# Attention with the values stationary and the turned exponentials moving, in a four-block kernel on one core

## The chip, the core and the metric

The kernel runs on one core of one Trainium2 chip. The core has TensorE (PE in the profile; its weight loads are listed as PEld and overlap it), VectorE (DVE), ScalarE (ACT), GpSimd (POOL) and SyncE (SP), each with its own instruction stream; they meet at semaphores. Matmuls write to PSUM, which has eight banks of 128 partitions by 512 words. The metric is the device time of one execution in microseconds (us).

## The reference, cut to what matters

The program computes a short gated convolution block with its MLP, an even block (attention beside a pooling path), a feed-forward block, a conformer block and another feed-forward block, on 512 positions of 1024 channels, all in float32. The change is inside the even block's attention, which has 8 heads of 64 channels and a decay that depends on the position:

```python
def forgetting_attention(q, k, v, f_logit, q_g, k_g):
    q = rms_norm(q, q_g); k = rms_norm(k, k_g)
    c = jnp.cumsum(jax.nn.log_sigmoid(f_logit), axis=1)
    ...
        s = einsum("bhqd,bhkd->bhqk", q_blk, k_h) * scale
        s = s + cq_blk[..., :, None] - c_k[:, :, None, :]
        s = where(k_pos <= q_pos, s, -inf)
        p = softmax(s, axis=-1)
        return einsum("bhqk,bhkd->bhqd", p, v_h)

def even_mixer(h, ...):
    ...
    return concatenate([a_out, p_out], axis=-1) @ w_out
```

## The kernel before, in words

Channels lie on partitions and positions on the free axis, except in attention, where a block of 128 queries lies on partitions. Weights come in units of 1024 x 256 in float32. ACT rounds each unit to a high half (`hi_half`, two copies of 128x1024 a unit), DVE computes the low half (`lo_half`), and PE forms three products for each (high x high, high x low, low x high). Attention itself runs in plain float32, for which PE issues two weight loads and two matmuls where the program has one.

All engines follow orders written out by hand. The attention stage is a loop of steps `s`, four to a head: step `s = 4h + q` is query block `q` of head `h`, and the causal mask leaves `(q + 1) * 128` keys to it. I call the steps q0 to q3, and the last block's turned exponentials "block q3". The stages are pipelined by hand over the steps:

- PE (lines 1837 to 1879): at step s the scores of s (stationary QS, moving KS, L1851) and the mask (L1852) into one of three banks; the turning of the exponentials of step s-2, block by block of 128 keys, by transposes into bank 4 or 5 (L1860); the product with V of step s-3 (L1871), in which the turned exponentials are stationary and V's 64 columns move, `q + 1` matmuls for a step, into bank 6 or 7. At four steps a pool product (L1879) follows.
- DVE (L1360 to L1383): the row minimum of step s (L1362; the scores are negated), a reciprocal of the sum (L1365), and the scaled output copied to `OT` (L1370). For heads 2 to 7 it also scales the queries and keys (`scaled_head`, L1306 and L1308), two full operations a head.
- ACT (L750 to L785): the copy of the turned exponentials from PSUM to `PT` (L756), the exponential with the row sum as a by-product (L771, an ACTIVATE and a read of the accumulator), for heads 2 to 7 the decay rows of queries and keys (`decay_rows`, L747 and L748: one partition of 512), and copies for the pooling path (L781).

After the loop PE runs the first four chunks of one output unit (24 matmuls, L1896 to L1898), turns `OT` by 16 transposes (L1907) so that channels lie on partitions again, and goes on with the output projection; ACT and DVE split the turned result into halves `HH` and `HL` (L785, L1383).

Which order the engines keep is the text of these loops; a wait names the count of another engine's semaphore. ACT and DVE work through their own lists in order, so an instruction that waits holds up all behind it.

Of the kernel before, what the change touches and what calls it, by code (L numbers as in the profile page):

```python
# [27 lines left out]
P = 128  # L28
T = 512
# [89 lines left out]

SUMMED_BY_PE = (ST_X0, ST_X1, ST_X2)  # L120
# [18 lines left out]
S_BANKS, POOL_BANK = (0, 1, 2), 3  # L139


def program(nc, i, out):
    ctx = ExitStack()
    with ctx:
# [12 lines left out]
        OT = at("OT", 16, [P, TB, T])  # L157
# [22 lines left out]
        V = at("V", 164.5, [P, TB, T])  # L180
# [11 lines left out]
        QS = at("QS", 172.5, [97, 2, T])  # L192
        KS = at("KS", 176.5, [97, 2, T])
        PR = at("PR", 180.5, [P, 2, T])
        PT = at("PT", 188.5, [P, 2, T])
# [59 lines left out]
        a_qk, a_row = sem("head_qk"), sem("head_decay_rows")  # L255
        a_s, a_min, a_e, a_rr = (sem("attn_" + x) for x in ("scores", "min", "exp", "recip"))
        a_t, a_tc, a_o, a_oe = (sem("attn_" + x) for x in ("turned", "copied", "out", "out_copied"))
        a_ot, a_h = sem("attn_out_turned"), sem("attn_out_hi")
# [31 lines left out]
        def first_unit(u, i):  # L290

            k = slice(2 * i, 2 * i + 2)
            if u < 2:
                return RAW[:, 1 - u, k, :], WH[:, 1 - u, k, :], WL[:, 1 - u, k, :]
            return RAW_3[:, k, :], WH_3[:, k, :], WL_3[:, k, :]

# [4 lines left out]
        def _(sp):  # L301
# [119 lines left out]

# [36 lines left out]
        def _(pool):  # L458
# [54 lines left out]

            pool.wait_ge(a_s, 8 * (HEADS // 2))
# [40 lines left out]
        def _(act):  # L555
# [194 lines left out]
            def turned_exponentials(k):  # L750

                n = (k % 4 + 1) * P
                act.wait_ge(a_t, k + 1)
                if k >= 2:
                    act.wait_ge(a_o, k - 1)
                act.activation(PT[:, k % 2, 0:n], PS_[:, 4 + k % 2, 0:n], ACT.Copy).then_inc(a_tc, 1)  # L756

            decay_rows(0)
            decay_rows(1)
            act.wait_ge(s_rc, 1)  # L760
            act.wait_ge(s_mm, U_EVEN + 8)
            for b in (2, 3):
                act.activation(V[:, b, UW:2 * UW], PS_[:, 3, b % 2 * UW:b % 2 * UW + UW], ACT.Copy, scale=sc_(S_RT + b)
                               ).then_inc(s_vr, 1)
            for s in range(4 * HEADS + 2):
                if s >= 2:
                    turned_exponentials(s - 2)
                if s < 4 * HEADS:
                    n = (s % 4 + 1) * P
                    act.wait_ge(a_min, s + 1)  # L770
                    act.activation(PR[:, s % 2, 0:n], PS_[:, S_BANKS[s % 3], 0:n], ACT.Exp, scale=-1.0,  # L771
                                   bias=sc_(S_MN + s % 8), accum_out=sc_(S_RS + s % 8)).then_inc(a_e, 1)
                if s == 3 or s == 6:
                    hi_half(U_EOUT + 1, 1, s // 6)
                if s % 4 == 1 and 5 <= s < 4 * HEADS - 4:
                    decay_rows(s // 4 + 1)
                if s % 4 == 3 and 11 <= s < 27:
# [172 lines left out]
        def _(dve):  # L950
# [43 lines left out]
            def split(m, gs=None, gain=None, k=0):  # L994
# [8 lines left out]
                for c in range(DC):  # L1003
# [307 lines left out]
            for p in range(8):  # L1311
# [16 lines left out]
                else:  # L1328
                    dve.wait_ge(s_rc, 1)
                    for b in range(TB if p == 6 else 2):  # L1330
                        ins = dve.tensor_scalar(V[:, b, (p - 6) * UW:(p - 5) * UW],
                                                PS_[:, 2 * j + b // 2, b % 2 * UW:b % 2 * UW + UW], sc_(S_RT + b), None,
                                                ALU.mult)
# [24 lines left out]
            for s in range(4 * HEADS + 4):  # L1358
# [4 lines left out]
                if 2 <= s < 4 * HEADS + 2:  # L1363
                    dve.wait_ge(a_e, s - 1)
                    dve.reciprocal(sc_(S_RR + (s - 2) % 8), sc_(S_RS + (s - 2) % 8)).then_inc(a_rr, 1)  # L1365
                if s >= 4:
                    k = s - 4
                    dve.wait_ge(a_o, k + 1)
                    dve.wait_ge(a_rr, k + 1)
                    dve.tensor_scalar(OT[:, k % 4, k // 4 * DH:k // 4 * DH + DH], PS_[:, 6 + k % 2, 0:DH],  # L1370
                                      sc_(S_RR + k % 8), None, ALU.mult).then_inc(a_oe, 1)
# [9 lines left out]
            for c in range(4):  # L1381
                dve.wait_ge(a_h, c + 1)
                tt(HL[:, c, :], PS_[:, 4 + c, :], HH[:, c, :].bitcast(F32), ALU.subtract).then_inc(s_x, 1)  # L1383
# [714 lines left out]
```

## Time and profile before

| | |
|---|---|
| Median of 3 runs | 1735.19 us (1731.91, 1735.19, 1735.36) |
| The profiled execution | 1731.89 us, span 1730.1 us |
| PE busy | 1709.8 us, 99% of the span |
| DVE, ACT, POOL busy | 1090.4, 693.2, 153.9 us |
| Attention, first score load to last product with V | 701.7 to 756.3 us of the span |
| DMA | 176.22 MB, mean 102 GB/s |

"Busy" for PE includes a modelled tail of each matmul, so that a busy PE can still have waited. The distance between the starts of two instructions tells more: a block that issues every 0.22 us although each matmul is listed with 0.39 us is a pipelined one. The granted clock of PE is given in parts of its full speed.

### The profile page before, as it was taken

What the parts mean: (1) busy time and instruction counts of PE and PEld (TensorE: products, weight loads), DVE (VectorE), ACT (ScalarE), POOL (GpSimd) and SP (SyncE); (2) the same over time, 40 slices, a digit from 0 to 9 for tenths busy, and PEclk for the clock granted to TensorE, in tenths of its full rate; (3) what the DMA queues carried; (4) which work ended last, traced back from release to release, by engine and by line L of the source; (5) the groups of instructions that cost most, each with busy time, mean ns of one, the idle gap of its engine ahead of it and who ended that gap; (6) DMA issues with size and microseconds to landing.
All of it is one profiled execution on the core that took longest, in us unless ns stands there. A gap on an engine that the chain in (4) does not pass through costs nothing.

```text
span 1730.1 us, 21548 instructions
## 1 busy us (share of the span) xinstructions
PE 1709.8 (99%) x7716; PEld 1382.4 (80%) x7716; DVE 1090.4 (63%) x1657; ACT 693.2 (40%) x1006; POOL 153.9 (9%) x142
## 2 busy tenths in 40 slices
PE   8999999999999999999999999999999999999999
PEld 7888878888888778888888888877656888888888
DVE  6799885353535573746663663669998666366364
ACT  4322353232323334744432432447666443243242
POOL 0000300000000040000000000005892000000000
PEclk9999999999999999999999999999999999999999
DMA  8566414323333132103232232232210323223222
GB/s 292 180 222 221 140 50 146 98 97 97 116 97 98 49 90 82 49 1 100 97 111 82 97 102 93 85 109 73 74 49 25 111 96 110 76 96 113 80 85 86
DMA packets 182338, 176.22 MB, mean 102 GB/s; under 512 B 3304, under 2 KB 181740, under 8 KB 182268
## 3 DMA queue, kind: packets, MB, share of 16 engines
q1 hardware_dynamic: 182268, 175.29, 31.7%
q8 instruction: 43, 0.70, 0.2%
q14 instruction: 27, 0.22, 0.0%
HBM read 173.15 MB, written 2.10 MB: 101 GB/s over the span
## 4 chain that ended last, share of the span: by engine, by line
PE 88%; DVE 9%; issue 1%; ACT 1%; DMA 1%; SPq 0%; DVEq 0%; ACTq 0%
PE PSUM L1546 23%; PE PSUM L1547 23%; PE PSUM L1548 23%; DVE PSUM L1478 4%; DVE WL L957 1%; PE PSUM L1871 1%; PE PSUM L1851 1%; PE PSUM L1896 1%; PE PSUM L1898 1%; PE PSUM L1897 1%; PE PSUM L1578 1%; PE PSUM L1632 1%; PE PSUM L1579 1%; PE PSUM L1580 1%; PE PSUM L1663 1%
## 5 line engine op out<-in xcount | busy, mean ns | idle before, releaser
L564 ACT ACTIVATE WH<-RAW 128x1024 fp32r<-128x1024 f32 x274 | 281.5, 1052 | 733.8 <-PE PSUM L1548 690.7
L1546 PE MATMUL PSUM<-XH,WH 128*128 128x512 f32 x1152 | 450.3, 391 | 0.0
L1548 PE MATMUL PSUM<-XH,WL 128*128 128x512 f32 x1152 | 448.2, 389 | 0.0
L1547 PE MATMUL PSUM<-XL,WH 128*128 128x512 f32 x1152 | 448.2, 389 | 0.0
L957 DVE TENSOR_TENSOR WL<-RAW,WH 128x1024 fp32r<-128x1024 f32 x274 | 341.3, 1268 | 10.5 <-ACT WH L564 10.5
L1546 PEld LDWEIGHTS PSUM<-XH,WH 128*128 128x128 f32 x1152 | 216.2, 188 | 46.2 <-issue 1.2
L1547 PEld LDWEIGHTS PSUM<-XL,WH 128*128 128x128 f32 x1152 | 216.2, 188 | 45.7 <-issue 1.2
L1548 PEld LDWEIGHTS PSUM<-XH,WL 128*128 128x128 f32 x1152 | 216.2, 188 | 45.1
L1546 PE MATMUL PSUM<-HH,WH 128*128 128x512 f32 x644 | 251.3, 390 | 0.4
L1548 PE MATMUL PSUM<-HH,WL 128*128 128x512 f32 x644 | 250.6, 389 | 0.0
L1547 PE MATMUL PSUM<-HL,WH 128*128 128x512 f32 x644 | 250.6, 389 | 0.0
L1401 DVE TENSOR_TENSOR ZP<-PSUM,R 128x512 f32<-128x512 f32 x88 | 56.7, 687 | 176.7 <-PE PSUM L1548 176.7
L1546 PEld LDWEIGHTS PSUM<-HH,WH 128*128 128x128 f32 x644 | 120.9, 188 | 27.5 <-DVE HL L1425 2.1
L1548 PEld LDWEIGHTS PSUM<-HH,WL 128*128 128x128 f32 x644 | 120.9, 188 | 25.2
L1547 PEld LDWEIGHTS PSUM<-HL,WH 128*128 128x128 f32 x644 | 120.9, 188 | 24.8
L524 POOL TENSOR_TENSOR CP<-CP,PRD 128x512 f32<-128x512 f32 x69 | 94.5, 1370 | 446.3 <-ACT PRD L908 437.4
L1042 DVE TENSOR_TENSOR X<-PSUM,X 128x512 f32 (+1 forms) x62 | 39.9, 685 | 146.1 <-PE PSUM L1548 114.0
L1412 DVE SCALAR_TENSOR_TENSOR TA<-ZP,VCOL,TA 128x512 f32<-128x512 f32 x176 | 120.2, 745 | 0.0
L1478 DVE SCALAR_TENSOR_TENSOR PSUM<-UPAD,VCOL,PSUM 128x512 f32<-128x512 f32 x123 | 83.4, 749 | 0.4
L1247 DVE TENSOR_SCALAR TA<-PSUM 128x512 f32<-128x512 f32 x32 | 20.6, 686 | 80.2 <-PE PSUM L1548 78.5
L992 DVE SCALAR_TENSOR_TENSOR MACC<-ARAW,small,MACC 128x256 f32<-128x256 f32 x140 | 67.9, 485 | 5.0
L825 ACT ACTIVATE TA<-ZP,VCOL 128x512 f32<-128x512 f32 x88 | 66.5, 802 | 0.2 <-issue 0.2
(336 smaller groups left out, 2001.6 us busy)
## 6 DMA issues: line engine op xcount, KB each, us to landing
RAW<-in_ffn_w_up SPq DMA_DIRECT2D x44, 1024.0 KB, 5.0
ARAW<-in_ada_w SPq DMA_DIRECT2D x24, 1024.0 KB, 5.3
RAW<-in_mlp_w_in SPq DMA_DIRECT2D x16, 1024.0 KB, 5.2
RAW<-in_mlp_w_out SPq DMA_DIRECT2D x16, 1024.0 KB, 4.9
RAW<-in_ffn_w_down SPq DMA_DIRECT2D x16, 1024.0 KB, 5.0
RAW<-in_sc_w_in SPq DMA_DIRECT2D x9, 1024.0 KB, 5.1
RAW<-in_even_w_in SPq DMA_DIRECT2D x8, 1024.0 KB, 5.5
RAW<-in_odd_w_pw SPq DMA_DIRECT2D x16, 512.0 KB, 5.3
```

The costliest lines, as they stand in the source:

```text
L524: pool.tensor_tensor(CP[:, n, :], CP[:, n, :], PRD[:, before % RING, :], ALU.add).then_inc(g_a, 1)
L564: act.activation(WH[:, j, a:b, :], RAW[:, j, a:b, :], ACT.Copy).then_inc(s_hi, 1)
L825: act.activation(TA[:, c, :], ZP[:, c, 2:T + 2], ACT.Identity, scale=col(f"fw{layer}2", it * 2 + (half + 2 * first + c)), bias=col(f"fb{la ...
L957: tt(WL[:, j, a:b, :], RAW[:, j, a:b, :], WH[:, j, a:b, :].bitcast(F32), ALU.subtract).then_inc(s_lo, 1)
L992: stt(dst, w, s, dst, ALU.mult, ALU.add).then_inc(s_as if k < 7 else s_ad, 1)
L1042: ins = dve.tensor_copy(d, src) if first else tt(d, src, d, ALU.add)
L1401: tt(ZP[:, c, 2:T + 2], banks(j, c), R[:, :], ALU.mult).then_inc(f_z, 1)
L1412: stt(TA[:, c, :], ZP[:, c, tap:tap + T], col(f"fw{layer}{tap}", it * 2 + (half + 2 * first + c)), TA[:, c, :], ALU.mult, ALU.add).then_in ...
L1478: stt(acc, src, w, acc, ALU.mult, ALU.add).then_inc(g_v, 1)
L1546: pe.matmul(o, wh, mh[:, k, :], start=(k == 0), stop=False)
L1547: pe.matmul(o, wh, ml[:, k, :], start=False, stop=False)
L1548: mm = pe.matmul(o, wl, mh[:, k, :], start=False, stop=(k == kn - 1))
```

## The change

The product with V is turned round. For each head there are now four matmuls instead of ten: V and 64 columns of ones are stationary (`VA`, 128x128), and the turned exponentials move, 512, 384, 256 and 128 of them for the four key blocks. The result has 64 partitions of output channels and 64 partitions of row sums, for all 512 queries of the head. The reciprocal of the sums is made on ACT as Exp(-Ln(sum)) for a whole head, DVE multiplies it in, and the result already has channels on partitions. So the sixteen transposes and `OT` go, and the halves `HH` and `HL` are made from `ON` inside the loop. The decay rows are written by DMA from SP instead of ACT; the exponential no longer reads the accumulator; the smallest of the four turned copies (128 keys) goes from ACT to DVE. `PT` now holds two whole heads.

```diff
-            def decay_rows(n):
-                act.wait_ge(e_cr, 32)
-                act.wait_ge(a_qk, 2 * n + 2)
-                act.activation(QS[64:65, n % 2, :], CR[64:65, n, :], ACT.Copy).then_inc(a_row, 1)
-                act.activation(KS[96:97, n % 2, :], CR[96:97, n, :], ACT.Copy).then_inc(a_row, 1)
...
@@ SP
+            def decay_rows(n):
+                if n >= 2:
+                    sp.wait_ge(a_s, 4 * n - 4)
+                sp.dma_start(QS[64:65, n % 2, :], CR[64:65, n, :]).then_inc(a_row[n % 2], 16)
+                sp.dma_start(KS[96:97, n % 2, :], CR[96:97, n, :]).then_inc(a_row[n % 2], 16)
...
+                    sp.wait_ge(e_cr, 32)
+                    sp.wait_ge(s_zero, 4)
+                    decay_rows(0)
+                    decay_rows(1)
...
             load(U_EOUT + 2, 0, eout, 2 * UW)
+            decay_rows(2)
+            decay_rows(3)
             load(U_EOUT + 3, 1, eout, 3 * UW)
+            for n in range(4, HEADS):
+                decay_rows(n)
@@ POOL
+            pool.wait_ge(s_f, 1)
+            pool.memset(VA[:, :, :, 1, :], 1.0).then_inc(a_one, 1)
@@ ACT
-            for s in range(4 * HEADS + 2):
-                if s >= 2:
-                    turned_exponentials(s - 2)
+            for s in range(4 * HEADS + 7):
+                if 2 <= s < 4 * HEADS + 2 and (s - 2) % 4:
+                    k = s - 2
+                    act.wait_ge(a_t, k + 1)
+                    if k >= 8:
+                        act.wait_ge(a_o, k // 4 - 1)
+                    act.activation(turned_step(k), PS_[:, 4 + k % 2, 0:(k % 4 + 1) * P]..., ACT.Copy).then_inc(a_tc, 1)
                 if s < 4 * HEADS:
                     n = (s % 4 + 1) * P
+                    if s >= 2:
+                        act.wait_ge(a_t, s - 1)
                     act.wait_ge(a_min, s + 1)
                     act.activation(PR[:, s % 2, 0:n], PS_[:, S_BANKS[s % 3], 0:n], ACT.Exp, scale=-1.0,
-                                   bias=sc_(S_MN + s % 8), accum_out=sc_(S_RS + s % 8)).then_inc(a_e, 1)
+                                   bias=sc_(S_MN + s % 8)).then_inc(a_e, 1)
                 if s == 3 or s == 6:
                     hi_half(U_EOUT + 1, 1, s // 6)
-                if s % 4 == 1 and 5 <= s < 4 * HEADS - 4:
-                    decay_rows(s // 4 + 1)
-                if s % 4 == 3 and 11 <= s < 27:
+                if s % 4 == 3 and s >= 7:
+                    n = s // 4 - 1
+                    sums, to = (slice(DH, P), slice(0, DH))[::1 - n % 2 * 2]
+                    act.wait_ge(a_o, n + 1)
+                    if n >= 4:
+                        act.wait_ge(a_on, n - 3)
+                    act.activation(RI[to, n // 2 % 2, :], PS_[sums, 6 + n % 2, :], ACT.Ln).then_inc(a_ln, 1)
+                    act.wait_ge(a_ln, n + 1)
+                    act.activation(RI[to, n // 2 % 2, :], RI[to, n // 2 % 2, :], ACT.Exp, scale=-1.0).then_inc(a_ri, 1)
+                if s % 8 == 5 and s >= 13:
+                    c = s // 8 - 1
+                    act.wait_ge(a_on, 2 * c + 2)
+                    act.activation(HH[:, c, :], ON[:, c % 2, :], ACT.Copy).then_inc(a_h, 1)
+                if s % 4 == 2 and 10 <= s < 26:
...
@@ DVE
-                if 2 <= s < 4 * HEADS + 2:
-                    dve.reciprocal(...)
-                if s >= 4:
-                    dve.tensor_scalar(OT[...], PS_[:, 6 + k % 2, 0:DH], sc_(S_RR + k % 8), ...)
+                if s % 4 == 2 and s < 4 * HEADS:
+                    k = s - 2
+                    dve.wait_ge(a_t, k + 1)
+                    dve.tensor_copy(turned_step(k), PS_[:, 4 + k % 2, 0:P]...).then_inc(a_td, 1)
+                if s % 4 == 0 and s >= 8:
+                    n = s // 4 - 2
+                    dve.wait_ge(a_ri, n + 1)
+                    tt(ON[mine, n // 2 % 2, :], PS_[mine, 6 + n % 2, :], RI[mine, n // 2 % 2, :], ALU.mult)...
+                if s % 8 == 6 and s >= 14:
+                    c = s // 8 - 1
+                    dve.wait_ge(a_h, c + 1)
+                    tt(HL[:, 4 + (c + 1) % 4, :], ON[:, c % 2, :], HH[:, c, :].bitcast(F32), ALU.subtract)...
@@ PE
-                if s >= 3:
-                    k = s - 3
-                    pe.wait_ge(a_tc, k + 1)
-                    for b in range(k % 4 + 1):
-                        mm = pe.matmul(PS_[:, 6 + k % 2, 0:DH], PT[:, k % 2, b * P:b * P + P],
-                                       V[:, b, k // 4 * DH:k // 4 * DH + DH], ...)
+                if s % 4 == 2 and s >= 6:
+                    n = s // 4 - 1
+                    ...
+                    pe.wait_ge(a_tc, copied_by_act(4 * n + 4))
+                    pe.wait_ge(a_td, copied_by_dve(4 * n + 4))
+                    for b in range(TB):
+                        mm = pe.matmul(PS_[:, 6 + n % 2, b * P:T], VA[:, b, n // 2, n % 2:n % 2 + 2, :],
+                                       turned_keys(n, b), start=(b == 0), stop=(b == TB - 1), ...)
+                    mm.then_inc(a_o, 1)
-                if s % 4 == 2 and 10 <= s < 26:
+                if s % 4 == 1 and 9 <= s < 25:
...
-            for c in range(4):
-                for b in range(TB):
-                    pe.transpose(PS_[:, 4 + c, b * P:b * P + P], OT[:, b, c * P:c * P + P], ...)
```

The same stretch of PE's list, one head's worth of it from a middle head on, first before the change, from the scores of q0 to the last product of that head's predecessor (q3 of the head before is turned at q1):

```order
L1851 MATMUL PSUM<-KS,QS 128x128
L1852 MATMUL PSUM<-MASK,IDENT 128x128
L1860 MATMUL PSUM<-IDENT,PR 128x128 x3
L1871 MATMUL PSUM<-V,PT 128x64 x2
L1851 MATMUL PSUM<-KS,QS 128x256
L1852 MATMUL PSUM<-MASK,IDENT 128x128
L1860 MATMUL PSUM<-IDENT,PR 128x128 x4
L1871 MATMUL PSUM<-V,PT 128x64 x3
L1851 MATMUL PSUM<-KS,QS 128x384
L1852 MATMUL PSUM<-MASK,IDENT 128x128
L1860 MATMUL PSUM<-IDENT,PR 128x128
L1871 MATMUL PSUM<-V,PT 128x64 x4
```

There the product with V follows the turning at each step, two, three or four matmuls of 64 columns. The same place of PE's list after the change:

```order
L1893 MATMUL PSUM<-KS,QS 128x128
L1894 MATMUL PSUM<-MASK,IDENT 128x128
L1904 MATMUL PSUM<-IDENT,PR 128x128 x3
L1893 MATMUL PSUM<-KS,QS 128x256
L1894 MATMUL PSUM<-MASK,IDENT 128x128
L1904 MATMUL PSUM<-IDENT,PR 128x128 x4
L1893 MATMUL PSUM<-KS,QS 128x384
L1894 MATMUL PSUM<-MASK,IDENT 128x128
L1904 MATMUL PSUM<-IDENT,PR 128x128
L1917 MATMUL PSUM<-PT,VA 128x512
L1917 MATMUL PSUM<-PT,VA 128x384
L1917 MATMUL PSUM<-PT,VA 128x256
```

The products with V stood between the scores of every step; now they stand in one piece, between the turning of q0 and the scores of q3, and nothing stands between q3's scores and q1's, except turnings and q0's scores.

ACT's list in a middle head, before, from the turned copy of q1's exponentials at step q3 on (PT is a turned copy, PR an exponential, HHP a copy for the pooling path):

```order
L756 ACTIVATE PT<-PSUM 128x256
L771 ACTIVATE PR,small<-PSUM,small 128x512
L781 ACTIVATE HHP<-PSUM,VCOL 128x512
L756 ACTIVATE PT<-PSUM 128x384
L771 ACTIVATE PR,small<-PSUM,small 128x128
L756 ACTIVATE PT<-PSUM 128x512
L771 ACTIVATE PR,small<-PSUM,small 128x256
L747 ACTIVATE QS<-CR 1x512
L748 ACTIVATE KS<-CR 1x512
L756 ACTIVATE PT<-PSUM 128x128
L771 ACTIVATE PR,small<-PSUM,small 128x384
```

No Ln or Exp of sums stands there; the decay rows do. The same place of ACT's list after the change (RI is the reciprocal of the sums, L810 its Ln and L812 its Exp):

```order
L793 ACTIVATE PT<-PSUM 128x2x128
L800 ACTIVATE PR<-PSUM,small 128x512
L810 ACTIVATE RI<-PSUM 64x512
L812 ACTIVATE RI<-RI 64x512
L793 ACTIVATE PT<-PSUM 128x3x128
L800 ACTIVATE PR<-PSUM,small 128x128
L793 ACTIVATE PT<-PSUM 128x4x128
L800 ACTIVATE PR<-PSUM,small 128x256
L800 ACTIVATE PR<-PSUM,small 128x384
L821 ACTIVATE HHP<-PSUM,VCOL 128x512
```

Two full-width operations now stand between the exponential of q3 and the turned copies of q2 and q3, where before a copy for the pooling path stood in four heads and nothing in the others. The decay rows and the copy of q0 are gone from this list.

## Rows read from the trace of the kernel before

**Rows 1.** Page, parts 1, 5 and 6: busy time; a group; a DMA issue, its landing last
```profile
PE 1709.8 (99%) x7716; PEld 1382.4 (80%) x7716; DVE 1090.4 (63%) x1657; ACT 693.2 (40%) x1006; POOL 153.9 (9%) x142
...
L564 ACT ACTIVATE WH<-RAW 128x1024 fp32r<-128x1024 f32 x274 | 281.5, 1052 | 733.8 <-PE PSUM L1548 690.7
...
RAW<-in_even_w_in SPq DMA_DIRECT2D x8, 1024.0 KB, 5.5
```

**Rows 2.** Windows over the stage: us, busy of each engine, clock, DMA share, GB/s
```profile
703.96:710.40 6.44, 5.99 (x45) 4.95 (x43) 4.55 (x16) 5.97 (x17) 0.00 (x0) 1.00 0.01 3
...
710.40:751.36 40.96, 40.41 (x262) 31.92 (x262) 28.85 (x89) 33.29 (x90) 0.00 (x0) 1.00 0.08 27
```

**Rows 3.** Timeline of PE: start us, us, engine, line, operation, out<-in, count
```profile
710.40 1.08 PE L1851 MATMUL PSUM<-KS,QS 97*128 97x512 f32 x2
...
716.60 1.08 PE L1879 MATMUL PSUM<-UP,WP 128*128 128x512 f32 x2
...
717.51 1.02 PE L1851 MATMUL PSUM<-KS,QS 97*128 97x512 f32 x2
...
745.31 1.08 PE L1851 MATMUL PSUM<-KS,QS 97*128 97x512 f32 x2
...
751.36 1.08 PE L1851 MATMUL PSUM<-KS,QS 97*128 97x512 f32 x2
```

**Rows 4.** Timeline of weight loads, same columns, idle time before in brackets
```profile
747.54 0.52 PEld L1871 LDWEIGHTS PSUM<-V,PT 128*128 128x128 f32 x4 [0.26 <-issue]
...
749.59 0.30 PEld L1851 LDWEIGHTS PSUM<-KS,QS 97*128 97x128 f32 x2
...
750.35 0.14 PEld L1860 LDWEIGHTS PSUM<-IDENT,PR 128*128 128x128 f32 x1
...
750.41 0.97 PEld L1871 LDWEIGHTS PSUM<-V,PT 128*128 128x128 f32 x8
...
751.31 0.30 PEld L1851 LDWEIGHTS PSUM<-KS,QS 97*128 97x128 f32 x2
...
752.28 0.20 PEld L1860 LDWEIGHTS PSUM<-IDENT,PR 128*128 128x128 f32 x2 [0.24 <-issue]
```

**Rows 5.** Timeline behind the last score product, all engines
```profile
752.54 0.69 DVE L1362 TENSOR_REDUCE small<-PSUM 128x1 f32<-128x512 f32 x1 [1.12 <-PE PSUM L1852]
...
753.27 0.69 ACT L771 ACTIVATE PR<-PSUM,small 128x512 f32<-128x512 f32 x1
...
753.85 0.19 ACT L771 ACTIVATION_READ_ACCUMULATOR PR<-PSUM,small 128x1 f32 x1
...
754.79 0.60 ACT L756 ACTIVATE PT<-PSUM 128x512 f32<-128x512 f32 x1 [0.36 <-PE PSUM L1860]
...
755.44 0.97 PEld L1871 LDWEIGHTS PSUM<-V,PT 128*128 128x128 f32 x8 [0.21 <-ACT PT L756]
```

**Rows 6.** Timeline of ACT in a head with a pool product
```profile
727.66 0.49 ACT L756 ACTIVATE PT<-PSUM 128x384 f32<-128x384 f32 x1
...
728.03 0.38 ACT L771 ACTIVATE PR<-PSUM,small 128x128 f32<-128x128 f32 x1
...
728.28 0.22 ACT L771 ACTIVATION_READ_ACCUMULATOR PR<-PSUM,small 128x1 f32 x1
```

**Rows 7.** Timeline of ACT at a root: Ln, then Exp of its result
```profile
616.41 0.69 ACT L588 ACTIVATE R<-PSUM,small 128x512 f32<-128x512 f32 x1 [3.31 <-PE PSUM L1620]
...
617.13 0.63 ACT L590 ACTIVATE R<-R 128x512 f32<-128x512 f32 x1
```

**Rows 8.** Timeline of weight loads: the turned outputs and the next product
```profile
761.70 1.90 PEld L1907 LDWEIGHTS PSUM<-IDENT,OT 128*128 128x128 f32 x16
...
763.56 0.19 PEld L1896 LDWEIGHTS PSUM<-HHP,WH 128*128 128x128 f32 x1
```

**Rows 9.** Timeline of PE: one-column matmuls near the program's start
```profile
34.09 1.71 PE L1632 MATMUL PSUM<-small,ARAW 128*128 128x1 f32 x10
```

**Rows 10.** Windows: the stretch in which they stand, columns as rows 2
```profile
34.00:38.00 4.00, 4.00 (x20) 3.66 (x19) 2.82 (x7) 0.67 (x1) 0.00 (x0) 0.57 0.55 134
```

More of the change, by code:

```diff
@@ L117, in added_tap, with copied_by_act, copied_by_dve @@
     return scaled_tap(n, k) - n - 1
+def copied_by_act(k):
+    return k - (k + 3) // 4
+def copied_by_dve(k):
+    return (k + 3) // 4
 SUMMED_BY_PE = (ST_X0, ST_X1, ST_X2)
@@ L139 @@
 S_BANKS, POOL_BANK = (0, 1, 2), 3
+PT_HEAD = 3 * 384 + T
 def program(nc, i, out):
@@ L254, in program @@
         s_wp, e_mx, s_pm, e_ph = sem("pool_w"), sem("pool_mixed"), sem("pool_product"), sem("pool_hi")
[L255 to L258, printed above, removed]
+        a_qk, a_row = sem("head_qk"), [sem("decay_rows_even"), sem("decay_rows_odd")]
+        a_s, a_min, a_e, a_one = (sem("attn_" + x) for x in ("scores", "min", "exp", "ones"))
+        a_t, a_tc, a_td, a_o = (sem("attn_" + x) for x in ("turned", "copied_act", "copied_dve", "out_and_sums"))
+        a_ln, a_ri, a_on, a_h, a_x = (sem("attn_" + x) for x in ("sum_ln", "sum_recip", "out_scaled", "out_hi", "out_lo"))
         g_s, g_u, g_v, g_o, g_d, g_m = (sem("conf_" + x) for x in
@@ L762, in _ @@
             for b in (2, 3):
[L763 to L767 removed]
+                act.activation(VA[:, b, 2:4, 0:3:2, :], PS_[:, 3, b % 2 * UW:b % 2 * UW + UW].rearrange(
+                    "p (c e d) -> p c e d", e=2, d=DH), ACT.Copy, scale=sc_(S_RT + b)).then_inc(s_vr, 1)
@@ new lines, in _ @@
+            act.wait_ge(e_cr, 32)
+            act.wait_ge(e_mx, 4)
+            for s in range(4 * HEADS + 7):
[4 more added lines that the diff above has]
+                        act.wait_ge(a_o, k // 4 - 1)
+                    act.activation(turned_step(k), PS_[:, 4 + k % 2, 0:(k % 4 + 1) * P].rearrange("p (b n) -> p b n", n=P),
+                                   ACT.Copy).then_inc(a_tc, 1)
@@ L1356, in _ @@
                     scaled_head(1)
-            for s in range(4 * HEADS + 4):
+            dve.wait_ge(e_cr, 32)
+            for s in range(4 * HEADS + 7):
                 if s < 4 * HEADS:
@@ L1856, in _ @@
                     pe.wait_ge(a_e, k + 1)
-                    if k >= 2:
-                        pe.wait_ge(a_tc, k - 1)
+                    if k >= 2 and k % 4 == 2:
+                        pe.wait_ge(a_td, copied_by_dve(k - 1))
+                    elif k >= 2:
+                        pe.wait_ge(a_tc, copied_by_act(k - 1))
                     for b in range(k % 4 + 1):
@@ L1891, in out_chunk @@
                         pe.wait_ge(s_ev, u - 1)
-                pe.wait_ge(s_x, 24 + n + 1)
+                if n < 4:
+                    pe.wait_ge(s_x, 24 + n + 1)
+                else:
+                    pe.wait_ge(a_x, n - 3)
                 for c in range(2):
@@ L1900, in out_chunk @@
                     mm.then_inc(s_mm, 1)
-            for n in range(4):
-                out_chunk(U_EOUT, n)
-            pe.wait_ge(a_oe, 32)
-            for c in range(4):
-                for b in range(TB):
-                    pe.transpose(PS_[:, 4 + c, b * P:b * P + P], OT[:, b, c * P:c * P + P], IDENT[:, :].bitcast(F32)
-                                 ).then_inc(a_ot, 1)
-            for n in range(4):
-                out_chunk(U_EOUT + 1, n)
+            for u in (U_EOUT, U_EOUT + 1):
+                for n in range(4):
+                    out_chunk(u, n)
             for u in (U_EOUT, U_EOUT + 1):
@@ L2068, in _ @@
             keep_busy(5, TAP_BANKS[1][1])
-            two_units(U_PW2, HH, HL, 48, n_h, 1)
+            two_units(U_PW2, HH, HL, 44, n_h, 1)
             for j in range(2):
-                product(U_PW2 + 2 + j, j, HH, HL, 8, s_x, 48)
+                product(U_PW2 + 2 + j, j, HH, HL, 8, s_x, 44)
             feed_forward(1)
```

82 lines of the change are left out of this document (38 added, 44 removed).

## The prediction

> **What bounds the kernel now.** I read the page first: PE is busy for 99% of the span, DVE for 63%, ACT for 40% [rows 1]. So time goes only where PE's list changes or where PE is made to wait. The window of the stage comes next. From the first q3 scores to the last ones it lasts 6.44 + 40.96 = 47.40 us, with ACT busy 5.97 + 33.29 = 39.3 us and the clock at 1.00 [rows 2]: here ACT is close behind PE. The starts of the q3 scores, which are the windows' borders too, give the length of a head: 6.44 us for the first, 751.36 - 745.31 = 6.05 for the last, and 717.51 - 710.40 = 7.11 for one with a pool product, which itself takes 0.91 from its start to the next scores [rows 2, 3]. In the last head the one gap listed is 0.26 [rows 4], so PE has 5.79 us of work in a head and waits little. Behind the last scores a chain runs from scores to minimum, exponential, copy and product [rows 5].
>
> **PE's own work.** A product of 128 columns more costs 0.21 us in plain float32: the scores of q2 with their mask take 750.35 - 749.59 = 0.76 and those of q3 0.97 [rows 4]. The old product of q3 takes 751.31 - 750.41 = 0.90 for four blocks, 0.225 a block, so ten blocks cost 2.25 a head [rows 4]. The new product moves 512 + 384 + 256 + 128 = 1280 columns, ten times 0.21, plus a few hundredths where a short one waits for its load: I take 2.13. PE's work falls only from 5.79 to 5.67. The real saving is the sixteen transposes behind the loop, 763.56 - 761.70 = 1.86 us, straight off PE's list [rows 8].
>
> **The ring that closes.** Before, each step's short product stood between one step's scores and the next, and covered the waits. Now follow the list from the load of q3's scores, counting from 0. To the minimum 1.23 [rows 4, 5]; to the exponential of q3 0.73; to the next ACT operation 0.58 [rows 5]. That next operation is now the Ln of the previous head's sums. Its product is long done, so it goes at once. Ln to Exp is 617.13 - 616.41 = 0.72 [rows 7]. The Exp lasts 0.63 [rows 7]; neighbours on ACT overlap by 0.12 (a copy of 0.49 us is followed after 0.37, rows 6), so 0.51. Then come the copy of q2, 0.37, the exponential of the next q0, 0.25 [rows 6], and the copy of q3: from its start to the product's load 0.65 [rows 5]. The product needs just this copy. It takes 2.13, and the next q3 scores stand behind it on PE. Sum: 1.23 + 0.73 + 0.58 + 0.72 + 0.51 + 0.37 + 0.25 + 0.65 + 2.13 = 7.17 us a head. PE's own 5.67 is shorter, and with the pool product, 6.58, too: that product now hides in the ring's wait. So ACT and the order of its list set the head's length, not its busy time.
>
> **Sum over the heads.** The first head has no Ln, but a `hi_half` in its place, 1.05 on the mean [rows 1] less the overlap, 0.93: 7.17 - 0.72 - 0.51 + 0.93 = 6.87 against 6.44, +0.43. The other six rings are 6 x 7.17 = 43.02 against 40.96, +2.06 [rows 2]. In two of them, with `HH`'s copy, the copy for the pooling path and DVE's splits all present, ACT reaches the exponential of q3 late. The whole copy would cost 0.51 each [rows 7], full cover nothing; I take 0.24, +0.48 for both. Tail: before, 755.44 - 751.31 = 4.13 to the last product, 0.90 for it [rows 4, 5] and the 1.86 of transposes: 6.89. After, the ring without the exponential of a next head: 7.17 - 0.25 = 6.92, +0.03. The change comes to 0.43 + 2.06 + 0.48 + 0.03 = +3.0 us. On the profiled execution's 1731.89 that is 1734.9; on the median 1735.19, which stands 3.3 above it, 1738.2. I predict 1738.
>
> **Edits at nothing.** The decay rows by DMA: a row's slot is free when the head two before has its last scores, a whole head (7 us) ahead of need. No row of this trace shows so small a transfer's landing; it is between nothing and the excess over those 7 us. A whole megabyte of weights lands in 5.5 us [rows 1], so a row queued behind one still comes in time, and I take nothing; with that cover gone each late us would be one of PE. The extra waits of SP sit ahead of a load that is held by an earlier unit's low half in any case. Gone are the read of the accumulator, the reciprocals and scaled outputs, and ACT's copy of q0; except for that read, already left out of the 0.58 and 0.25 above, none of them is in the ring. The new DVE product of 64x512 holds up the minimum of q1, but q1's exponential is next needed behind the 2.13 product. `HH` and `HL` of the last head have 24 chunks' matmuls before them. The memset of ones is on an idle POOL. The strided writes of `VA` and of the turned copies keep their element counts; at worst they cost twice a copy, at best nothing, and I take nothing.
>
> **A rule on the clock.** The row shows the granted clock at 0.57, the 1.2 GHz level, in 34 to 38 us [rows 10], where PE had just run matmuls of one column [rows 9]; in the attention stage, where PE's busy 5.99 of 6.44 us in the first head shows waits too, it stays at 1.00, the 2.4 GHz level [rows 2]. The ring leaves PE about 1.5 us of wait in a head without a pool product, in two or three pieces. The Trainium skill (TensorE: Matmul & The Clock Gate, A second HAM failure mode: psum-queue depth-cycling) says that frequent short idles between groups of matmuls can make the clock swing between its two levels; by it the product and the scores of q3, 3.1 us of the ring, would take twice that in the heads where it happens. By that rule the time would be some 19 us more, as the third rival has it; by the row, nothing.
>
> **The rivals.**
> 1. PE stays the bound and the ring is hidden. For it: PE's 99%. Against: the copy of q3 stands behind Ln and Exp in ACT's list and the product must wait for it. Price: seven heads at 5.67 and four pool products at 0.91 are 43.3 against 47.4; the tail without Ln and Exp is 4.13 + 2.13 = 6.26 against 6.89. Together -4.7 us: 1730.5.
> 2. The ring is longer, and the kernel clearly slower. Place: the hand-overs on ACT between the exponential of q3 and the copy of q3. If each of its operations with a wait starts only when the one before has ended, the 0.12 of overlap goes five times, 0.6 a head, 3.6 in six: +6.6, 1741.8. It decides from 0.08 us a ring on, since then the sum passes 3.5 us. For it: the exponential now carries a second wait, and the Ln two. Against: copy and exponential, which wait too, overlap [rows 6].
> 3. The clock falls in the six rings: 6 x 3.1 = 18.6 on top, 1757. For it: rows 9 and 10, and longer waits. Against: rows 2.
> 4. The rows by DMA come late, so that the work taken off ACT comes back on PE: 1 us in each of six heads is +6, 1744. Against: the 7 us of room.
>
> **How the numbers follow.** About 0.2%, 3.5 us, is what a measurement of this kernel can tell from no change. The forecast, +1.5 to +5 around +3.0, has 0.66; rival 1 has 0.09, rival 2 0.17, rival 3 0.03, rival 4 0.05. Within the forecast 0.46 lie below +3.5 us and 0.20 above. The part of rival 1 that passes -3.5 is 0.08, the rest joins "same"; a sixth of rivals 2 and 4 falls short of +3.5 as well and joins it. So: faster 0.08, same 0.50, slower 0.42. The likeliest case's own range is 1736.5 to 1740. The range reaches toward rival 1 and takes in rival 2; the three runs themselves span 3.4 us, so it starts at the lower level of the runs plus one: 1733 to 1743, with 2 in 10 outside.
>
> **What would show it.** Right: the q3 scores start 7.1 to 7.4 us apart in every head, those without a pool product among them; PE waits before the turning of q0 and before the new product, with ACT's copy of q3 as releaser; Ln starts 0.6 behind the exponential of q3, and the next Ln waits for nothing. The new product takes 2.1 to 2.2 us. Wrong: heads without a pool product under 6.3 us; PE waiting for a DMA at the scores of q0; a clock under 1.00 in the stage; a new product well over 2.2 us; any shift after the first output chunks beyond the stage's own.

## The result and the profile after

The kernel after takes 1759.99 us, the median of 4 runs (1757.15 to 1760.37), against 1733.55 us for the kernel before (1731.79 to 1735.36, 4 runs): ratio 1.0152, 95% interval 1.014 to 1.0164. It is slower by 26 us, where the prediction said 3 and had 1743 as the upper end of its range. The profiled execution has a span of 1758.1 us against 1730.1, and it is that difference of 28.0 us that I account for below.

The page of the kernel after, parts 1 and 2, to be read beside [rows 1]:

```profile
PE 1722.1 (98%) x7604; PEld 1380.6 (79%) x7604; DVE 1088.9 (62%) x1609; ACT 688.4 (39%) x966; POOL 154.7 (9%) x143
...
PEclk8999999999999999889999999999999999999999
```

PE has 112 instructions fewer, by the forecast less work, and is busy for 12 us more. That points to slower work: the granted clock has two 8s in the middle, at slices 17 and 18, where attention stands; before, both are 9s. DVE and ACT do slightly less than before, so none of the 28 us is more work for them.

The stage is next. The timeline of PE, kernel after, with only the first scores of each q3 and the pool products; the columns and the use of the starts are as in [rows 3]:

```profile
705.87 1.02 PE L1893 MATMUL PSUM<-KS,QS 97*128 97x512 f32 x2
713.02 1.02 PE L1893 MATMUL PSUM<-KS,QS 97*128 97x512 f32 x2
716.16 1.02 PE L1925 MATMUL PSUM<-UP,WP 128*128 128x512 f32 x2
720.47 1.02 PE L1893 MATMUL PSUM<-KS,QS 97*128 97x512 f32 x2
727.43 2.05 PE L1925 MATMUL PSUM<-UP,WP 128*128 128x512 f32 x2 [3.65 <-DVE HLP L1424]
733.91 1.02 PE L1893 MATMUL PSUM<-KS,QS 97*128 97x512 f32 x2
...
747.45 1.02 PE L1893 MATMUL PSUM<-KS,QS 97*128 97x512 f32 x2
...
761.05 1.02 PE L1893 MATMUL PSUM<-KS,QS 97*128 97x512 f32 x2
768.52 1.02 PE L1893 MATMUL PSUM<-KS,QS 97*128 97x512 f32 x2
776.12 1.02 PE L1893 MATMUL PSUM<-KS,QS 97*128 97x512 f32 x2
```

The heads last 7.15, 7.45, 13.44, 13.54, 13.60, 7.47 and 7.60 us, 70.25 in all against 47.40. Four of them lie within 0.45 us of the forecast 7.17; three take nearly twice that. The three are those whose pool product is not the first. That product waits 3.65 us for `HLP`, the low half of the previous pool product, which DVE writes at L1424. The list of waits of PE from 700 to 787 us says the same in its first line (us in total, times, longest):

```profile
PE PSUM L1925 <- DVE HLP L1424: 11.0, 3, 3.7
```

Why `HLP` is late stands in the timeline of the same head, ACT and DVE together:

```profile
723.09 0.59 ACT L810 ACTIVATE RI<-PSUM 64x512 f32<-64x512 f32 x1
...
723.71 0.63 ACT L812 ACTIVATE RI<-RI 64x512 f32<-64x512 f32 x1
...
724.37 0.69 DVE L1412 TENSOR_TENSOR ON<-PSUM,RI 64x512 f32<-64x512 f32 x1 [1.89 <-ACT RI L812]
...
725.09 0.74 DVE L1343 SCALAR_TENSOR_TENSOR QS<-QK,small,SQT 64x512 f32<-64x512 f32 x1
725.14 0.59 ACT L793 ACTIVATE PT<-PSUM 128x512 f32<-128x512 f32 x1
725.76 0.73 DVE L1345 SCALAR_TENSOR_TENSOR KS<-QK,VCOL,SQT 64x512 f32<-64x512 f32 x1
726.53 0.75 DVE L1424 SCALAR_TENSOR_TENSOR HLP<-PSUM,VCOL,HHP 128x512 fp32r<-128x512 f32 x1
```

In DVE's list at q0 the new scaled output `ON` (L1412) comes first. It waits 1.89 us for the roots on ACT, and `scaled_head`'s two operations and `HLP` stand behind it, though they need no root. The copy of q3 that the product with V needs is done at 725.14 + 0.59 = 725.73, and a product could start there. Instead PE waits until 727.43, runs the pool product, the scores of q2 and a transpose, and only then the product.

The windows of that head show the second half of the loss; columns as [rows 2]:

```profile
720.47:723.50 3.03, 2.82 (x20) 2.07 (x18) 1.73 (x3) 2.13 (x5) 0.00 (x0) 1.00 0.32 91
723.50:727.40 3.90, 0.27 (x3) 0.04 (x2) 2.97 (x5) 2.15 (x5) 0.00 (x0) 0.80 0.59 199
727.40:731.00 3.60, 3.57 (x7) 1.96 (x8) 0.31 (x2) 0.99 (x2) 0.00 (x0) 0.50 0.00 0
```

The column reads 0.80 over the wait, so that the clock fell before the wait was over, and behind it the clock is 0.50, the 1.2 GHz level. The pool product takes 2.05 where it took 1.02 in the row at 716.16, and the product with V takes 3.21 in place of the 2.42 of the head before. In [rows 2] the same column reads 1.00 in the whole stage.

The end of attention, timeline of PE, kernel after, behind the last q3 scores at 776.12, to be read beside [rows 4, 5, 8]:

```profile
778.77 0.66 PE L1904 MATMUL PSUM<-IDENT,PR 128*128 128x128 f32 x4 [1.01 <-ACT PR L800]
781.10 4.61 PE L1917 MATMUL PSUM<-PT,VA 128*128 128x512 f32 x8 [1.67 <-DVE ON L1412]
785.36 0.78 PE L1945 MATMUL PSUM<-HHP,WH 128*128 128x512 f32 x1
```

(The `ON` for which this product waits is an earlier head's; what came last was ACT's pair of copies, which ended at 781.00.) Two waits, 1.01 and 1.67 us, and then the last product takes 4.61. The transposes of [rows 8] are gone, as they should be, but from the last q3 scores to the first output chunk there are 9.24 us. The kernel before has 6.85 for this and the transposes.

### The profile page after: what moved, and what is told of

Same layout as the page of the kernel before. It is cut to its first block, busy times and chain, and to the rows that moved or that the text cites. A ratio compares the mean times of both kernels' runs of the same rounds, so it can differ in the third digit from the quotient of the medians.

```text
span 1758.1 us, 21222 instructions
## 1 busy us (share of the span) xinstructions
PE 1722.1 (98%) x7604; PEld 1380.6 (79%) x7604; DVE 1088.9 (62%) x1609; ACT 688.4 (39%) x966; POOL 154.7 (9%) x143
## 4 chain that ended last, share of the span: by engine, by line
PE 87%; DVE 9%; issue 2%; ACT 1%; DMA 1%; SPq 0%; DVEq 0%; ACTq 0%
PE PSUM L1588 23%; PE PSUM L1590 23%; PE PSUM L1589 23%; DVE PSUM L1520 4%; PE PSUM L1917 1%; DVE WL L994 1%; PE PSUM L1945 1%; PE PSUM L1947 1%; PE PSUM L1946 1%; PE PSUM L1893 1%; PE PSUM L1620 1%; PE PSUM L1674 1%; PE PSUM L1621 1%; PE PSUM L1622 1%; PE PSUM L1705 1%
```

## The experiments

My theory, A in the expectations: the moved pool product waits for `HLP` behind the roots, and PE's idleness then lowers its clock; the ring of the prediction is right apart from its sizes. The chief rivals: the ring itself is this long, and the wait is only where it shows; or the clock falls by the short waits that every ring has. Each expectation spells out the rivals that its run is to tell apart.

**1. `HLP` ahead of the roots.** On DVE, in the changed kernel, the low half is moved up in q0, ahead of `ON` and `scaled_head`:

```diff
+                if s % 4 == 0 and 12 <= s < 28:
+                    g = s // 4 - 3
+                    dve.wait_ge(e_ph, g + 1)
+                    stt(HLP[:, POOL_TILES[g], :], PS_[:, POOL_BANK, :], ...).then_inc(s_x, 1)
                 if s % 4 == 0 and s >= 8:
                     n = s // 4 - 2
...
                     dve.wait_ge(a_ri, n + 1)
                     tt(ON[mine, ...], ...).then_inc(a_on, 1)
...
-                if s % 4 == 0 and 12 <= s < 28:
...
-                    stt(HLP[:, POOL_TILES[g], :], ...).then_inc(s_x, 1)
```

> The changed kernel with one block of DVE's list moved: at q0 the low half of the pool product (HLP) comes before the scaled output (ON) that waits for Ln and Exp. Theory A (the pool product, moved a step earlier, waits for a low half that is queued behind ON, and the clock falls behind that wait): the three heads of 13.5 us become 7.2 to 7.5 us, the clock of the stage is 1.00, and the time is 1738 to 1742 us. Rival B (the ring through Ln and Exp alone lets the clock fall, as the rule on frequent short idles would have it): the clock still falls in the stage and the time stays above 1750 us.

Measured: 1740.86 us (1739.29 to 1740.89), ratio to before 1.0046, interval 1.0028 to 1.0064; span 1737.5. The place of one DVE operation was worth some 18 of the 26 us. The windows of its stage and of its last product:

```profile
704.37:756.72 52.35, 47.61 (x221) 30.70 (x219) 34.08 (x64) 36.77 (x72) 0.00 (x0) 1.00 0.07 21
...
761.70:765.40 3.70, 3.70 (x8) 2.16 (x9) 0.00 (x0) 0.00 (x0) 0.00 (x0) 0.57 0.02 4
```

The seven heads last 7.15, 7.46, 7.60, 7.47, 7.60, 7.47 and 7.60, at a clock of 1.00, with a pool product or without: it hides in the ring, as forecast. So the ring itself is not 13.5 us long, and its own short waits don't lower the clock. What stays of the clock's fall is the last product, at 0.57. The ring itself, timeline of one head of this kernel:

```profile
718.87 0.30 PEld L1893 LDWEIGHTS PSUM<-KS,QS 97*128 97x128 f32 x2
...
720.11 0.89 DVE L1400 TENSOR_REDUCE small<-PSUM 128x1 f32<-128x512 f32 x2 [0.28 <-PE PSUM L1894]
...
720.89 0.69 ACT L800 ACTIVATE PR<-PSUM,small 128x512 f32<-128x512 f32 x1 [0.18 <-DVE small L1400]
...
721.61 0.59 ACT L810 ACTIVATE RI<-PSUM 64x512 f32<-64x512 f32 x1
...
722.23 0.63 ACT L812 ACTIVATE RI<-RI 64x512 f32<-64x512 f32 x1
...
722.88 0.49 ACT L793 ACTIVATE PT<-PSUM 128x384 f32<-128x384 f32 x1
...
723.40 0.37 ACT L800 ACTIVATE PR<-PSUM,small 128x128 f32<-128x128 f32 x1
...
723.66 0.59 ACT L793 ACTIVATE PT<-PSUM 128x512 f32<-128x512 f32 x1
...
724.32 0.30 PEld L1917 LDWEIGHTS PSUM<-PT,VA 128*128 128x128 f32 x2 [0.37 <-issue]
...
726.47 0.30 PEld L1893 LDWEIGHTS PSUM<-KS,QS 97*128 97x128 f32 x2
```

Its steps are 1.24, 0.78, 0.72, 0.62, 0.65, 0.52, 0.26, 0.66 and 2.15, in sum 7.60. The order is the forecast's, step for step. Too small were the step from the exponential to Ln (0.58 forecast, 0.72 here), from Exp to the copy (0.51 and 0.65) and from the copy to the exponential (0.37 and 0.52); Ln to Exp was too large by 0.10. The last of the three is too small only in the rings of 7.60, in the others it is 0.38 to 0.39 (715.43 to 715.82 in the same timeline), and that is the whole difference between 7.47 and 7.60.

**2. The wait filled with matmuls.** In the changed kernel PE runs four unused 512-column matmuls into a free bank where it waits. They change no wait on another engine, only what PE does meanwhile; their result is not used:

```diff
                     if g:
+                        pe.wait_ge(a_on, g)
+                        keep_busy(4, 6 + (g + 1) % 2)
                         pe.wait_ge(s_x, 24 + g)
```

> The changed kernel with four filler matmuls of 512 columns (3.4 us, result unused, into the bank of the next product) ahead of the pool product in the three heads where it waits; the wait for the low half stays. Theory A: the product still starts about 7 us behind the scores of q3, but the clock in those heads stays at 1.00, so each head takes 10.9 us instead of 13.5: 8 us less than the changed kernel, 1750 to 1753 us. If the clock falls for another reason (the form of the new product, or the ring's waits), the heads stay near 13.5 us and the time near 1760 us.

Measured: 1751.28 us (1750.4 to 1752.3), ratio 1.0108, interval 1.0089 to 1.0127; span 1748.8. The window of the first of its three long heads; the other two read the same, with 10.83 and 10.81 us:

```profile
720.47:731.29 10.82, 10.48 (x42) 5.92 (x41) 6.28 (x11) 6.44 (x13) 0.00 (x0) 1.00 0.29 98
```

The wait is as long as ever, the clock stays at 1.00, and the three heads take 32.46 us where the kernel after needs 40.58. So the clock costs 8.1 us there. The same heads in experiment 1 take 22.67; the wait itself, with the pool product and the scores of q2 that come out from under the ring, costs the other 9.8. This separates the two halves with one kernel.

**3. The ring with one copy more.** Experiment 1 plus one unused copy of 128x512 on ACT behind the roots:

```diff
                     act.activation(RI[to, n // 2 % 2, :], RI[to, n // 2 % 2, :], ACT.Exp, scale=-1.0).then_inc(a_ri, 1)
+                    act.activation(SPARE[:, :], VCOL[:, 0:T], ACT.Copy)
```

> As e1, with one more ACT copy of 128x512 (result unused) behind the Exp of the sums, in every head: it costs 0.51 us between the exponential of q3 and the copy of q3. Theory of the ring: each of six heads and the tail grow by 0.5 us, 3.0 to 3.6 us over e1. Rival (PE or DVE sets the head's length): no difference above 0.5 us.

Measured: 1742.34 us (1742.03 to 1743.83), ratio 1.0057, interval 1.0038 to 1.0076; span 1740.6, 3.1 above experiment 1's, but the median only 1.5 above: experiment 1's profiled execution was its fastest, and the two measures disagree on the size. The heads grew from 52.35 to 55.00 us, in six rings by 0.50 or 0.38, 0.44 on the mean; all six now last 7.96 to 7.98. ACT's list does set the length of a head. Part of the inserted operation was swallowed, as its timeline shows:

```profile
738.00 0.59 ACT L811 ACTIVATE RI<-PSUM 64x512 f32<-64x512 f32 x1
738.62 0.63 ACT L813 ACTIVATE RI<-RI 64x512 f32<-64x512 f32 x1
739.27 0.63 ACT L814 ACTIVATE SPARE<-VCOL 128x512 f32<-128x512 f32 x1
739.81 0.47 ACT L794 ACTIVATE PT<-PSUM 128x384 f32<-128x384 f32 x1
```

The added copy has no wait at all and still starts 0.65 behind an Exp of 0.63. Behind the added copy the next operation starts after 0.54 of 0.63. So a wait is not what takes the overlap away behind the Exp; there rival 2 of the prediction had the place right and the reason wrong. (In every other head it is the other way round: at 714.71 the added copy starts 0.54 behind its Exp, and the next operation 0.62 behind the added copy. The heads alternate in the half of the partitions that Ln reads and Exp writes, and in the `HH` copy; which of the two decides isn't shown.)

**4. The decay rows by DMA, alone.** Put into the kernel before: `decay_rows` from ACT to SP, as in the change, and nothing else.

```diff
+                sp.dma_start(QS[64:65, n % 2, :], CR[64:65, n, :]).then_inc(a_row[n % 2], 16)
+                sp.dma_start(KS[96:97, n % 2, :], CR[96:97, n, :]).then_inc(a_row[n % 2], 16)
...
-                act.activation(QS[64:65, n % 2, :], CR[64:65, n, :], ACT.Copy).then_inc(a_row, 1)
-                act.activation(KS[96:97, n % 2, :], CR[96:97, n, :], ACT.Copy).then_inc(a_row, 1)
```

> The kernel before with the decay rows by DMA from SP instead of ACT, nothing else. My reading: ACT is not the bound there, the rows land long before they are needed, and the time is 0 to 1 us lower than before (1732.5 to 1734). Rival (late rows): PE waits for a DMA at the scores of q0 in heads 2 to 7 and the time is above 1737 us.

Measured: 1733.56 us (10 runs), ratio 1.0003, interval 0.9991 to 1.0015. The q3 scores of head 0 and of head 7 stand at 704.17 and 751.44, 47.27 apart against 47.40. The rows cost nothing and, before, gain nothing.

**5. The roots off the ring.** Experiment 1, with Ln, Exp, `ON`, `HH` and `HL` later: the roots stand behind the exponential of q1, while PE runs the product with V.

```diff
-                if s % 4 == 3 and s >= 7:
-                    n = s // 4 - 1
+                if s % 4 == 1 and 9 <= s < 41:
+                    n = s // 4 - 2
...
-                if s % 8 == 5 and s >= 13:
-                    c = s // 8 - 1
+                if s % 8 == 2 and s >= 18:
+                    c = s // 8 - 2
```

> As e1, with Ln and Exp of the sums moved from step q3 to the end of step q1 of the next head, the scaled output on DVE to q2, and the halves of a pair of heads one and two steps later. Theory of the ring: what stands between the exponential of q3 and the copy of q3 falls by the two operations, 1.27 us by the starts in e1; heads without a pool product go from 7.5 to about 6.1 us, those with one to about 7.1 (PE's own order), and the last product runs at full clock. Sum 47.7 us over seven heads against 52.4 in e1 and 47.4 before; the time is 1731 to 1734 us, no difference from the kernel before. Rival (the ring isn't what sets the heads' length): 1738 us or more.

Measured: 1733.48 us (12 runs) against 1733.45, ratio 1.0005, interval 0.9996 to 1.0013. The first head lasts 7.15 us as ever, those with a pool product 6.98 to 7.33, the last two 6.28 and 6.27, and the seven 47.98, 4.4 below experiment 1. Its last product, in the timeline of PE:

```profile
753.11 0.66 PE L1904 MATMUL PSUM<-IDENT,PR 128*128 128x128 f32 x4 [1.02 <-ACT PR L800]
754.50 2.39 PE L1917 MATMUL PSUM<-PT,VA 128*128 128x512 f32 x8 [0.73 <-issue]
756.65 0.48 PE L1945 MATMUL PSUM<-HHP,WH 128*128 128x512 f32 x1
```

With the roots away from the last copies the second wait is 0.73 in place of 1.67, and the product takes 2.39: no fall of the clock here. The tail is 756.65 - 750.46 = 6.19 us against 6.85 before. Heads +0.58 and tail -0.66 add up to nothing, as the medians do.

**6. The pool product inside the ring's wait.** Experiment 5, with the pool product ahead of PE's turning of q3 and `HLP` on DVE one step earlier.

```diff
@@ DVE
-                if s % 4 == 0 and 12 <= s < 28:
-                    g = s // 4 - 3
+                if s % 4 == 3 and 11 <= s < 27:
+                    g = s // 4 - 2
@@ PE
+                if s % 4 == 1 and 9 <= s < 25:
+                    ...
+                    pe.matmul(PS_[:, POOL_BANK, :], WP[:, g, :], UP[:, g, 16:], start=True, stop=True).then_inc(s_pm, 1)
                 if 2 <= s < 4 * HEADS + 2:
                     k = s - 2
...
-                if s % 4 == 1 and 9 <= s < 25:
```

> As e5, with the pool product ahead of the turning of q3 at step q1 (where PE waits 0.45 us for the exponential of q3) and its low half on DVE at step q3. If PE's order sets those heads, they fall from 7.1 to 6.6 us, 2 us in all: 1729 to 1732 us, 1 to 3 us below the kernel before. If ACT's or DVE's list sets them, nothing changes against e5.

Measured: 1733.37 us (11 runs), ratio 0.9999, interval 0.999 to 1.0007. Seven heads 47.90 us, tail 6.19. The pool product fills one wait, but waits itself for `HLP`, 0.18 to 0.30 us in three heads. Nothing is gained over experiment 5, and neither beats the kernel before.

**7. The pool product one step earlier in the kernel before.** PE's pool product from q2 to q1, ACT's copy of it from q3 to q2: this is the change's move without the change.

```diff
@@ ACT
-                if s % 4 == 3 and 11 <= s < 27:
+                if s % 4 == 2 and 10 <= s < 26:
@@ PE
-                if s % 4 == 2 and 10 <= s < 26:
+                if s % 4 == 1 and 9 <= s < 25:
```

> The kernel before with only the pool product moved from step q2 to q1 and its high half from q3 to q2, as in the change. There the low half on DVE doesn't stand behind an Exp; it ends 4.8 us behind the load of q3's scores, and the product would reach the head of PE's list at 4.1: a wait of 0.7 to 0.8 us in each of three heads, clock at 1.00: 2 us slower at most, 1732 to 1736 us. If the moved product alone makes the damage, it is over 1745 us.

Measured: 1735.09 us (10 runs), ratio 1.0012, interval 1.0003 to 1.0021. PE's waits from 704 to 753 us:

```profile
PE PSUM L1879 <- DVE HLP L1379: 0.8, 3, 0.4
```

Three waits again and for the same tile, but 0.8 us in all and a clock of 1.00; the seven heads last 48.10, +0.7. The expectation had 0.7 to 0.8 for each of them, so this was a miss in size. The dependence was already tight. It is the roots in front of it on DVE that turn 0.2 to 0.45 us into 3.65.

**8. The pool product back in its old place in the changed kernel.** The reverse of 7: product at q2, copy at q3, `HLP` still behind the roots.

```diff
@@ ACT
-                if s % 4 == 2 and 10 <= s < 26:
+                if s % 4 == 3 and 11 <= s < 27:
@@ PE
-                if s % 4 == 1 and 9 <= s < 25:
+                if s % 4 == 2 and 10 <= s < 26:
```

> The changed kernel with the pool product back at step q2, behind the product with V, and its high half back at q3; ON still ahead of the low half on DVE. Theory A: the low half is ready long before, no wait of 3.65 us is left, the clock stays at 1.00, but the product now lies inside the ring: pool heads of 8.2 to 8.6 us, 1742 to 1746 us. Rival (the order of ON and the low half on DVE does the damage wherever the product stands): 1755 us or more.

Measured: 1747.85 us (1746.59 to 1751.2, 4 runs), ratio 1.0091, interval 1.0074 to 1.0109. PE no longer waits for `HLP`, but the ratio is 0.0045 above experiment 1's, some 8 us. Heads last 8.31, 8.89, 10.83, 10.39, 8.05 and 7.58 after the first. Theory A had the clock at 1.00 and 1742 to 1746 us here, and both were misses. Windows of the head that begins at 730.18:

```profile
730.18:734.00 3.82, 3.33 (x22) 2.44 (x20) 0.94 (x3) 1.96 (x4) 0.00 (x0) 1.00 0.02 3
734.00:736.00 2.00, 0.73 (x4) 0.26 (x2) 1.60 (x3) 1.98 (x5) 0.00 (x0) 1.00 0.00 0
736.00:738.00 2.00, 1.80 (x3) 0.84 (x3) 1.97 (x5) 0.47 (x2) 0.00 (x0) 0.54 0.00 0
738.00:740.00 2.00, 2.00 (x6) 1.23 (x5) 0.28 (x2) 0.76 (x2) 0.00 (x0) 0.60 0.04 8
```

And why PE was idle there, from the timelines of ACT and PE:

```profile
734.36 0.69 ACT L821 ACTIVATE HHP<-PSUM,VCOL 128x512 fp32r<-128x512 f32 x1
...
735.74 0.33 PE L1904 MATMUL PSUM<-IDENT,PR 128*128 128x128 f32 x1 [1.27 <-ACT PR L800]
736.27 4.04 PE L1917 MATMUL PSUM<-PT,VA 128*128 128x512 f32 x8 [0.20 <-issue]
```

The pool path's copy `HHP` now stands between the roots and the copy of q2, so the ring is longer by it; and the pool product is no longer under the ring but on top of it, 0.86 us (740.15 to 741.01). PE waits 1.27 us on end, and the product takes 4.04 us in place of 2.39.

The same kernel also shows such waits without a fall. Timeline of PE, a later head and the tail:

```profile
756.68 0.33 PE L1904 MATMUL PSUM<-IDENT,PR 128*128 128x128 f32 x1 [1.27 <-ACT PR L800]
757.21 2.40 PE L1917 MATMUL PSUM<-PT,VA 128*128 128x512 f32 x8 [0.20 <-issue]
...
769.68 0.66 PE L1904 MATMUL PSUM<-IDENT,PR 128*128 128x128 f32 x4 [1.02 <-ACT PR L800]
772.01 2.39 PE L1917 MATMUL PSUM<-PT,VA 128*128 128x512 f32 x8 [1.67 <-DVE ON L1412]
```

Four heads have a wait of 1.26 or 1.27 us. In two the clock falls, in two it stays at 1.00. The tail has the very waits of experiment 1's, 1.02 and 1.67, and its product takes 2.39 where that one took 4.07. So the waits alone don't say whether the clock falls.

Moving the pool product earlier was thus right for this ring; what was lacking was the move of `HLP` with it.

## Why the prediction was wrong

The 28.0 us of the profiled executions, by the prediction's own terms:

| | us | shown by |
|---|---|---|
| the forecast: heads +2.97, tail +0.03 | 3.0 | |
| rings longer than forecast: 52.35 against 50.37 | 2.0 | experiment 1 |
| the wait for `HLP` in three heads | 9.8 | experiments 1, 2 |
| the clock behind that wait | 8.1 | experiment 2 |
| tail over 6.92, with the first output chunks at the low clock | 3.2 | rows at 781.10, 785.36 |
| start of the program, before the stage | 1.9 | windows from 20 to 30 us, below |

- **The step that failed** is the sentence on DVE's new product: it "holds up the minimum of q1", and I looked no further down DVE's list. Behind it stand `scaled_head` and `HLP`, and the moved pool product waits for `HLP`. An earlier sentence, "that product now hides in the ring's wait", is right only when its operand is there; experiment 1 makes it true. I had followed the added wait on ACT through all that is queued behind it, and the one on DVE to the first neighbour only.
- **Rival 3**, a falling clock, had 0.03, and its 1757 us lies close to the result by accident. It put the fall into all six rings. Experiment 1 has the same short waits in each ring, and a clock of 1.00 there. In the kernel after the falls came where PE had waited long: in the waits of 3.65 us, and in the tail. So the rule that the Trainium skill gives (TensorE: Matmul & The Clock Gate, A second HAM failure mode: psum-queue depth-cycling), short idles that swing the clock, was worth more than 0.03: experiment 8, with 0.49 and then 1.27 us of wait, shows the granted clock at 0.54 to 0.60 behind it. Two other heads of experiment 8 with a wait of 1.26 or 1.27 us, and all heads of experiments 1, 3 and 5 to 7, show waits where it does not happen.
- **The tail's term** (+0.03) compared lengths at full clock. Its ring came out: less the 1.55 us by which the last product of experiment 1 is over 2.15, the tail is 7.15, forecast 6.92. Experiment 8's tail, with the same two waits and the clock at 1.00, is 774.16 - 767.03 = 7.13. The missing 3.0 us are the clock, and whether it falls there is not settled by the waits: it did in the kernel after and in experiments 1 to 3, not in experiment 8.
- **The ring.** Its closing, its order on ACT, the hidden pool product, PE's product of 2.15 (2.13 forecast), and ACT rather than PE as the bound are all shown by experiments 1 and 3. Its size was 7.47 and 7.60 in place of 7.17, mainly from the two hand-overs at the roots, each 0.14 too small, and in the rings of 7.60 the 0.15 behind the copy of q2. Rival 2 had given those 0.6 a head; it was 0.36 on the mean. The 0.48 for crowded heads cannot be seen: heads with and without `HH` differ by 0.13. The first head lasted 7.15 for 6.87. Without the missed wait the time would have been inside the range, but not near the forecast: experiment 1's ratio says +8 us in 1732 for +3, clearly slower, and outside "same", which I held the likeliest.
- **Edits at nothing.** The decay rows: right (experiment 4). `HH` and `HL` of the last head, ones by POOL and the strided writes: the list of waits has none for the halves or the ones. It has 0.23 us for `VA`, as before for `V`, and DVE's writes to it last 476 ns as those to `V` did. It has one wait of 0.36 us for DVE's turned copy, in the first head, which is thus no clean ring.
- **The saving** of the sixteen transposes is real, but it is worth 0.66 us net, and only where the roots don't stand in the tail's copies (experiment 5): with them there the tail is 7.13 even at full clock, against 6.85.

The 1.9 us ahead of the stage need no part of the change: its first q3 scores stand at 705.87 here and at 702.48 to 705.87 in the others of the changed form, with the same code ahead of them, and at 703.96 to 704.17 in the three of the old form. PE's clock in the first 50 us differs between executions. The windows from 20 to 30 us, of the kernel before:

```profile
20.00:30.00 10.00, 10.00 (x62) 8.11 (x61) 6.33 (x14) 5.96 (x11) 0.00 (x0) 1.00 1.10 352
```

And of the kernel after, with 0.87 in the clock's column for 1.00:

```profile
20.00:30.00 10.00, 10.00 (x55) 7.24 (x54) 5.27 (x11) 4.26 (x8) 0.00 (x0) 0.87 1.09 353
```

Two things stay open. First, when two neighbours on ACT overlap: behind the Exp a wait is excluded by experiment 3, and since the added copy overlaps the Exp in every other head, neither the 64 partitions nor the writing in place decides alone. Second, what exactly decides that the clock falls after some waits and not after others of the same length. Whether some order of this change beats the kernel before was not found either; experiments 5 and 6 only equal it.

## What to carry to other kernels

When a change puts a wait on an engine that works in order, write down every instruction behind it up to the next one that is free to be late, and ask of each who waits for it, above all an instruction that the same change moved earlier. Compute such a wait twice, once in time and once for the case that the clock falls behind it: here three waits of 3.65 us cost 9.8 us themselves and 8.1 us more in slow matmuls. Roots of a result that isn't needed soon belong where their engine would be idle, not between a score and the copy that the next product needs; moving them was worth about 7 us (ratios 1.0046 and 1.0005, experiments 1 and 5), 1.6 of them in the tail by a clock that didn't fall.

## What the runs showed of the hardware

- The granted clock was 0.50 after PE had waited 3.65 us, and already 0.66 from 725.50 to 726.50, inside that wait (kernel after). It was 0.54 to 0.60 after waits of 0.49 and 1.27 us with 0.73 us of work in the 2.00 before its fall (experiment 8), and 0.57 after 1.02 and 1.67 us (tail of experiment 1). It stayed at 1.00 after the same 1.02 and 1.67 us in the tail of experiment 8, after 1.27 us in one of its heads (756.68), after 1.20 us in two heads of experiment 3 (748.57 and 756.55), and after 1.02 and 0.73 us (tail of experiment 5).
- Four unused matmuls of 512 columns, which take the place of most of a 3.65 us wait, kept it at 1.00 (experiment 2).
- On ACT an operation started 0.09 to 0.12 us before the end of the one ahead in most places (739.27 to 739.81 for 0.63). Where it reads what that one wrote, it started 0.02 to 0.04 us behind the end: Ln to Exp, with 64 partitions (0.62 for 0.59) and with 128 (0.72 for 0.69, [rows 7]). So it did from the exponential to Ln (0.72 for 0.69) in every ring, and from Exp to the independent copy of experiment 3 in every other head (0.65 for 0.63; 0.54 in the rest).
- A product of float32 with 1280 columns and four stationary tiles took 2.15 us from its first load to the next one's, against 2.25 estimated for the ten blocks of 64 columns that it replaces: turning it round gained PE 0.1 us a head.
